# A hybrid decoder layer on one core: the input projection of the prompt's second half moved from the opening in among the expert tokens

## What is computed

```
p = h @ w_in                                  # 1024 -> RWKV r,k,v,w,a,g | GDN q,k,v,z,b,a | gates
ya, ... = rwkv_branch(p_rw, ...)              # token shift, low-rank maps, recurrence over tokens
yb, ... = gdn_branch(p_gd, ...)               # causal_conv of 4 taps, silu, l2norm, delta rule in chunks
merged = gates[..., :D] * (ya @ w_branch_a) + gates[..., D:] * (yb @ w_branch_b)
x1 = layer_norm(alpha * x + merged @ w_out)
...
hpre = einsum('tkd,td->tk', u_tab[e_b], x_b)  # 128 experts a token
y = einsum('tk,tkd->td', g_b * gelu(hpre), v_tab[e_b])
x2 = layer_norm(alpha * x1 + y)
```

## Time and profile before

| | |
|---|---|
| median of 3 runs | 2156.61 us (2156.49 to 2164.32) |
| span of the profiled execution | 2167.9 us |
| TensorE busy | 1626.5 us, 75% |
| VectorE busy | 1336.0 us, 62% |
| ScalarE busy | 398.7 us, 18% |
| GpSimd busy | 1019.4 us, 47% |
| moved by DMA | 718.93 MB, 332 GB/s over the span |

### The profile page before, as it was taken

One profiled execution on the slowest core, in us unless ns is written; L12 is line 12 of the kernel. 1 busy time (PEld: TensorE's weight loads), 2 busy tenths in 40 slices (PEclk: granted clock), 3 DMA queues, 4 the chain that ended last, 5 costly groups with the idle time before them and its releaser, 6 DMA issues. The chain is left out here.

```text
span 2167.9 us, 32130 instructions
## 1 busy us (share of the span) xinstructions
PE 1626.5 (75%) x12765; PEld 974.2 (45%) x12789; DVE 1336.0 (62%) x2996; ACT 398.7 (18%) x754; POOL 1019.4 (47%) x1091
## 2 busy tenths in 40 slices
PE   7998879897978785598888656888776555656555
PEld 7887866864655552065655302666553000100000
DVE  4296177784645458865545777645456875676745
ACT  1321332241222011113401201223012000100000
POOL 0000020004645555665545566645455677777774
PEclk9997999996989996599999756979998555555555
DMA  9214286656999999999999999989999999999997
GB/s 253 77 49 136 80 223 183 225 177 225 358 369 400 399 401 407 377 355 388 394 399 400 412 403 382 383 304 398 399 400 404 401 402 405 406 406 397 406 407 273
DMA packets 271257, 718.93 MB, mean 332 GB/s; under 512 B 29220, under 2 KB 77823, under 8 KB 270075
## 3 DMA queue, kind: packets, MB, share of 16 engines
q0 software_dynamic: 151904, 554.59, 66.3%
q1 hardware_dynamic: 116552, 161.44, 21.7%
q10 hardware_dynamic: 2650, 0.85, 0.2%
HBM read 695.58 MB, written 21.30 MB: 331 GB/s over the span
## 5 line engine op out<-in xcount | busy, mean ns | idle before, releaser
L2558 DVE CUSTOM_DVE_ANT_0 arena<-arena,ps 128x1024 f32<-128x1024 f32 x520 | 634.5, 1220 | 523.1 <-PE ps L2611 331.7
L2458 POOL DMA_INDIRECT arena<-peer_u_dram,arena x520 | 503.2, 968 | 500.6 <-DVE arena L2558 415.9
L2503 POOL DMA_INDIRECT arena<-peer_v_dram,arena x520 | 489.0, 940 | 163.6 <-issue 152.5
L2611 PE MATMUL ps<-arena 48*128 48x512 bf16 x1040 | 264.7, 501 | 338.3 <-DVE arena L2558 325.6
L1318 PE MATMUL ps<-arena 128*128 128x128 f32 (+1 forms) x3072 | 415.7, 291 | 85.9 <-DMA arena<-w_in_dram 35.1
L1318 PEld LDWEIGHTS ps<-arena 128*128 128x128 f32 x3072 | 380.6, 200 | 178.7 <-issue 123.0
L2624 PE MATMUL ps<-arena 128*32 128x512 f32 x2080 | 397.1, 847 | 24.0 <-DMA arena<-peer_v_dram,arena 23.8
L2611 PEld LDWEIGHTS ps<-arena 48*128 48x128 bf16 x1040 | 53.7, 98 | 648.7 <-DVE arena L2558 574.0
L2592 ACT ACTIVATE arena<-arena 128x4 f32<-128x4 f32 x130 | 26.8, 206 | 910.1 <-DVE arena L2558 909.8
L388 PE MATMUL ps<-arena 128*128 128x260 f32 (+1 forms) x704 | 131.7, 349 | 3.9 <-ACT arena L466 3.9
L388 PEld LDWEIGHTS ps<-arena 128*128 128x128 f32 x704 | 116.4, 193 | 18.1 <-ACT arena L466 4.0
(11 more groups left out here) (367 smaller groups left out, 1805.6 us busy)
## 6 DMA issues: line engine op xcount, KB each, us to landing
arena<-w_in_dram SPq DMA_DIRECT2D x40, 1024.0 KB, 13.1
arena<-peer_wq_dram SPq DMA_DIRECT2D x32, 1024.0 KB, 14.6
arena<-w_out_dram SPq DMA_DIRECT2D x16, 1024.0 KB, 15.7
arena<-w_in_dram SPq DMA_DIRECT2D x30, 512.0 KB, 4.1
arena<-peer_u_dram,arena POOLq DMA_INDIRECT x520
arena<-peer_v_dram,arena POOLq DMA_INDIRECT x520
arena<-w_branch_a_dram SPq DMA_DIRECT2D x8, 1024.0 KB, 14.8
arena<-w_branch_b_dram SPq DMA_DIRECT2D x8, 1024.0 KB, 16.7
```

The costliest lines, as they stand in the source:

```text
L2458: pool.indirect_dma_start(m["arena"][:, at:at + D], None, m["a"]["peer_u"][0], offsets(m, k)).then_inc(m["sem"](f"e_u{k % RU // UB}"), 16)
L2503: pool.indirect_dma_start(e["V"][j % RV], None, a["peer_v"][0], offsets(m, j)).then_inc(v_in[j % RV // BATCH], 16)
L2558: dve.tensor_tensor_reduce(u, u, ps[:, 0:2, :], 1.0, 0.0, ALU.mult, ALU.add, e["hp"][:, c:c + 1]).then_inc(sem("e_h"), 1)
L2611: mm = pe.matmul(ps[:, h, :], e["pick"][r, i:i + 1].to_broadcast([3 * GROUP, P]), e["xp"][r, g % 2, :], start=True, stop=True)
```

## The change

The opening projects tiles 0 and 1 and the samples alone, 264 columns, for all 30 tiles of w_in. The late part of the opening goes. Instead the recurrence of tile 0 carries the transposes of x of tiles 2 and 3 and their small GDN inputs (`extra_pe` and its like), and the rest of the projection of tiles 2 and 3 is done in the running stage (`second_*`), 256 columns at a time: the 30 units stand 1.4 tokens apart from token 95 on, their weights come in 15 slabs of 512x512 through a ring of four, and the 11 results are written to `fin`, 22 transfers of 256 KB. Tile 2's recurrence begins at token 141 instead of 118, tile 3's at 249 instead of 244, and some paces of choosing and of the samples are set anew.

```diff
-BEGINS = (-160.0, 3.0, 118.0, 244.0)
-STRETCH = (1.0, 1.0, 1.0, 1.07)
-CHOOSE_PACE = (0.55, 0.58, 0.78, 0.78, 1.2)
+BEGINS = (-160.0, 3.0, 141.0, 249.0)
+STRETCH = (1.0, 1.0, 0.86, 1.02)
+CHOOSE_PACE = (0.4, 0.58, 0.56, 0.7, 1.2)
...
-                    pe.wait_ge(tile_out, i - 1)
-                few = TILES[i] >= RT_
-                for h in range(1 if few else 2):
-                    for k in range(KD):
-                        x = xA[:, k, :] if few else xT[:, k, h * TH:(h + 1) * TH]
-                        mm = pe.matmul(ps[:, 2 * (i % 2) + h, 0:NA if few else TH], ring[:, i % WS, k, :], x, start=(k == 0), stop=(k == KD - 1))
+                if i >= 4:
+                    pe.wait_ge(tile_out, i - 3)
+                for k in range(KD):
+                    mm = pe.matmul(ps[:, i % 4, 0:TA], ring[:, i % WS, k, :], xT[:, k, :], start=(k == 0), stop=(k == KD - 1))
...
-S_AT = dict(rows=33.2, save=38.6, exp=51.2, rw=46.6, gd=52.5, sum0=63.2, gd2=63.6, sum1=76.3, turn=78.5, keys=85.8)
+S_AT = dict(rows=33.2, save=36.0, exp=47.5, rw=44.0, gd=48.5, sum0=51.5, gd2=52.0, sum1=59.5, turn=61.0, keys=63.5)
...
+SB, UNIT = 95.0, 1.4
+SSLOTS = 4
+SECOND_SLABS = [(g, h) for g, n in GROUPS for h in range(1 if n == 2 else 2)]
+SPILLS = ("gk", "gq", "gv", "z", "gg", "A", "B", "R", "K", "bonus", "V")
...
+def second_sp(m, sp):
+
+    a, sem, f = m["a"], m["sem"], m["second"]
+    slabs = [sem(f"p_slab{i}") for i in range(SSLOTS)]
+
+    def slab(s):
+        g, h = SECOND_SLABS[s]
+        c0 = GROUP_ROW[g] * P
+        if s >= SSLOTS:
+            sp.wait_ge(sem("p_mm"), unit_number(SECOND_SLABS[s - SSLOTS][0], dict(GROUPS)[SECOND_SLABS[s - SSLOTS][0]] - 1))
+        if g == "wg":
+            src, here = a["w_in"][0, :, c0:c0 + 256], shaped(flat(f["ring"][s % SSLOTS]), [KD, 256])
         else:
-            pe.wait_ge(out, taken(u - 2))
-
-    def project_late(g):
+            src, here = a["w_in"][0, 512 * h:512 * h + 512, c0:c0 + 512], f["ring"][s % SSLOTS]
+        sp.dma_start(here, src.rearrange("(k p) c -> p k c", p=P)).then_inc(slabs[s % SSLOTS], 16)
...
+                if h == 0 and u > 2:
+                    pe.wait_ge(out, u - 2)
+                slot = f["ring"][s % SSLOTS]
+                for k in range(4):
+                    w = shaped(flat(slot), [KD, 256])[:, 4 * h + k, ct * P:(ct + 1) * P] if n == 2 else slot[:, k, ct * P:(ct + 1) * P]
+                    mm = pe.matmul(ps[:, FB + u % 2, 0:NF], w, f["x"][:, 4 * h + k], start=(h == 0 and k == 0), stop=(h == 1 and k == 3))
...
-            in_turn(recur_r_pe(m, pe, 0), recur_g_pe(m, pe, 0), front_pe(m, pe, 0), sample_pe(m, pe), late_pe(m, pe))
+            in_turn(recur_r_pe(m, pe, 0), recur_g_pe(m, pe, 0), extra_pe(m, pe), front_pe(m, pe, 0), sample_pe(m, pe))
-TURN = (116, 116, 116, 108)
+TURN = (116, 120, 116, 108)
...
 def fin_sp(m, sp, n):
 
     tn = tokens(n)
-    yield front_at(n - 1, "fin")
+    yield front_at(n - 1, "fin") if n > 2 else unit_at("v", 3) + 6.8
     m["fs"].wait(sp, n, "rows", 0)
+    if n == 2:
+        second_done(m, sp)
     sp.dma_start(m["finbuf"][:, 0:NFIN * tn], m["a"]["fin"][n - 1][:, 0:NFIN * tn]).then_inc(m["sem"]("fin_in"), 16)
...
-            in_turn(experts_sp(m, sp), *(s(m, sp, n) for n in later for s in (fin_sp, front_sp, store_sp) if (s, n) != (fin_sp, 1)), states_sp(m, sp), rows_sp(m, sp))
+            in_turn(experts_sp(m, sp), second_sp(m, sp), *(s(m, sp, n) for n in later for s in (fin_sp, front_sp, store_sp) if (s, n) != (fin_sp, 1)), states_sp(m, sp), rows_sp(m, sp))
...
-            in_turn(experts_dve(m, dve), *(s(m, dve, n) for n in later for s in (recur_r_dve, recur_g_dve, front_dve)),
+            m["second_steps"] = Steps(dve, sem("p_step"))
+            in_turn(experts_dve(m, dve), second_dve(m, dve), *(s(m, dve, n) for n in later for s in (recur_r_dve, recur_g_dve, front_dve)),
...
-            in_turn(experts_pe(m, pe), *(s(m, pe, n) for n in later for s in (recur_r_pe, recur_g_pe, front_pe)),
+            in_turn(experts_pe(m, pe), second_pe(m, pe), *(s(m, pe, n) for n in later for s in (recur_r_pe, recur_g_pe, front_pe)),
```

More of the change, by code:

```diff
@@ L216, in program @@
             m[name] = late.take(shape, dt)
[L217 to L232, removed]
+        m["arena"], m["rings_at"] = arena, late.at
+        small_at = expert_rows(m)[2]
+        fin_at = ARENA - NFIN * (P + NS)
+        high = Space(arena, small_at + SMALL, fin_at)
+        for name, n in (("Praw", RT_), ("sw", 4), ("aa", 4), ("G", 4), ("Gi", 4), ("mix", RT_), ("kk", 4), ("scr", 4), ("xT", KD), ("gg", 4),
+                        ("rawA", QT), ("sqA", 8), ("convA", QT), ("zA", ZT)):
+            m[name + "_at"] = high.at
+            m[name] = high.take([P, n, TA])
+        m["Gp"] = m["sw"]
+        m["once_at"] = high.at
+        m["finbuf"] = arena[:, fin_at:ARENA]
+        second = Space(arena, fin_at, ARENA)
+        for name, shape in (("xrowB", [P, 2, D]), ("xTB", [P, KD, NF]), ("wba", [P, KD, BG]), ("lin", [BG, NF]), ("spB", [BG, NF]), ("keep", [P, 2, NF])):
+            m[name] = second.take(shape)
+        early = Space(arena, low.at, small_at)
         m["tmp"] = lambda name, shape, dt=F32: early.take(shape, dt)
@@ L336, in _ @@
         def _(dve):
-            for n in range(NT):
+            for n in range(2):
                 dve.wait_ge(turned, n + 1)
@@ L1010, in recur_g_pe @@
     for h in range(HG):
-        mm = pe.matmul(by4(G + 1)[:, h], selv[0:BG, HG + h], i["bg"], start=True, stop=True)
+        mm = pe.matmul(by4(G + 1)[:, h], row(32 + h), i["bg"], start=True, stop=True)
     mm.then_inc(S_["selg"], 1)
@@ L1025, in recur_g_pe @@
     for h in range(HG):
-        mm = pe.matmul(by4(G + 1)[:, h], selv[0:BG, h], i["bg"], start=True, stop=True)
+        mm = pe.matmul(by4(G + 1)[:, h], row(h), i["bg"], start=True, stop=True)
     mm.then_inc(S_["selb"], 1)
@@ L1270, in front_sp @@
                 sp.wait_ge(m["sem"]("q_kmm"), 2)
-            elif before == "f":
+            else:
                 source, g, h = SLABS[j]
@@ L1707, in opening_buffers @@
+    m["samples"] = s
+    rest = Space(space.arena, own.at, end)
+    f.update(qT=rest.take([P, HP * P]), left=rest.take([P, D]), parts=rest.take([P, 3, D], BF16),
+             scores=shaped(past_mix, [HP, NK]), x1row=past_mix[:, HP * NK:HP * NK + D])
     f["choose"] = {}
@@ new lines, in chain, with merged, extra_pe @@
+def chain(*streams):
+    for s in streams:
+        yield from s
+def merged(*streams):
+    heads = [next(s, None) for s in streams]
+    while any(h is not None for h in heads):
+        i = min((i for i, h in enumerate(heads) if h is not None), key=lambda i: heads[i])
+        yield heads[i]
+        heads[i] = next(streams[i], None)
+def extra_pe(m, pe):
+    ps, sem = m["ps"], m["sem"]
+    yield begins(0) + 4.0
+    pe.wait_ge(sem("xB_in"), 32)
+    for n in range(2):
+        for k in range(KD):
+            mm = pe.transpose(ps[:, 2 * n + k // 4, (k % 4) * P:(k % 4 + 1) * P], m["xrowB"][:, n, k * P:(k + 1) * P], const(m, "ident"))
+            if k % 4 == 3:
+                if k == 7:
+                    mm.then_inc(sem("xB_mm"), 1)
+                yield begins(0) + 4.5 + 1.0 * n + 0.5 * (k // 4)
+    yield begins(0) + 8.0
+    pe.wait_ge(sem("xB_out"), 2)
+    for k in range(KD):
+        mm = pe.matmul(ps[0:BG, 0, 0:NF], m["wba"][:, k, :], m["xTB"][:, k, :], start=(k == 0), stop=(k == KD - 1))
+    mm.then_inc(sem("xB_ba"), 1)
@@ L2467, in clear_small @@
 def clear_small(m, dve):
+    yield begins(0) + 33.0
     e, sem = m["small"], m["sem"]
```

958 lines of the change are left out of this document (528 added, 430 removed).

## The result

The changed kernel is slower: a median of 2238.09 us (2234.73 to 2242.64) against 2160.47 us for the kernel before in the same runs, a ratio of 1.0352 with an interval of 1.0307 to 1.0397. That is 78 us more, where 26 were forecast and the range ended at 2215. The sign was right, the size was not.

What follows compares the result with a forecast made beforehand. The opening was taken as bound by TensorE, the running stage by memory bytes; -62 us in the opening and +88 running (57 + 19 + 8 + 4) gave +26, a median of 2183 us, range 2134 to 2215.

Steps and rivals of the forecast that it cites:

- Opening: Stretch up to the first expert token: loading, projecting, recurrence, front, choosing and end together save 62 us, between 45 and 80.
- Project: Opening's projection: fewer TensorE instructions at 264 columns, with TensorE staying the bound, -25 us (-18 to -32).
- Recurrence: Tile 0's recurrence in the opening: added transposes and matmuls on TensorE cost +10 us (+5 to +14).
- Front up to the first query's scores: Front of tile 0: late groups go, but TensorE waits for the samples' two sums and the keys, -23 us (-15 to -33).
- End: End of the opening: choosing without late work, -8 us, and first expert multiply no longer behind the last late group, -11.
- Bytes: Running stage: 23.1 MB of slabs, x, low-rank weights and spills at 403 GB/s, with no idle DMA to hide them, +57 us.
- +19 in tokens 94 to 116: Running stage: added convolutions and norms make VectorE the bound, +19 us beyond the bytes (0 to +30).
- +8 in 116 to 142: Running stage: TensorE, memory and VectorE near full and chained, +8 us (0 to +20).
- Tile 2's input: Running stage: tile 2's recurrence starts later and its input loads only after the last spill, +4 us (0 to +15).
- (a): Rival: rings of gathered rows absorb the VectorE and TensorE overload, so only bytes count; 2154 us, chance 0.2.
- (b): Rival: samples' chain does not limit the opening, second sum under 65 us after the recurrence; 2132 to 2145 us, chance 0.2.
- (c): Rival: SyncE's queue delays the second projection, pushing tile 2's recurrence and front into its choosing; 2213 us, chance 0.15.

Runs made afterwards that it cites:

- floor run: Changed kernel without the second projection's engine work, slabs, x, low-rank weights and the last states' outputs; only 22 spills of zeros stay: 2131.69 us.
- transfers-only run: Changed kernel without the second projection's work on TensorE, VectorE and ScalarE and the last states' outputs; its transfers stay, spilling zeros: 2174.36 us.
- run of rows alone: The transfers-only run without low-rank weights, plus VectorE's full-width second-projection rows on constants at their old places: 2209.40 us.
- Narrow rows: Changed kernel with nearly all second-projection rows on VectorE cut from 256 columns to 8 or less, zeros spilled: 2205.95 us.
- half of the matmuls: Changed kernel with 4 of 8 matmuls in each of the second projection's 30 units: 2234.32 us alone, 2199.82 us together with narrowed VectorE rows.

## Why the prediction was wrong

**Opening, -62 forecast, -54 measured.** Loading: the first projecting matmul starts at 16.04 us instead of 21.86, -6 (-5). Project: -15 (-25). The last of its main matmuls did come 30 us earlier (149.24 for 179.03, loading included), as the instruction count said; but then TensorE waited 14.43 us for VectorE ahead of the recurrence, where it had waited 3.14. The prediction let the two changes on VectorE cancel; the longer tail is the 10 us. Recurrence: -1 (+10); the added transposes found room in its waits. Front up to the first query's scores: -17 (-23). The mechanism was right: the first sum came 60 us after the front began (61 forecast), the second 88 (85). End: -15 (-19).

**Bytes, +57 forecast.** Right for 17.3 MB, which cost 43 us. For the 5.8 MB of spills, 14 us by the same price, no run shows the price alone: the floor run, which has them, lies 34 us under the kernel before where the opening alone gives 54, and the 20 between hold its wait of 30.0 us for tile 2's input, with tokens that went faster elsewhere.

**The work among the tokens, +19 in tokens 94 to 116 and +8 in 116 to 142: the step that failed.** By the floor runs the work costs 64 us over the transfers, where these two terms allowed 27. By the tokens' starts in the two traces, the changed kernel loses 22 us to the transfers-only run from token 94 to 95, 27 to token 116 and 33 to token 142; some 19 come back behind that, where the transfers-only run has the longer wait for tile 2's input. So the sum failed in three places.

At token 95 it had nothing. x was costed in bytes, not as a transfer that may start only when tile 1's rows have left its buffer, with TensorE and VectorE standing in order behind it. That stage took 27 us; without the wait it takes 5, as before. How much would come back if this wait alone went is not shown, since the runs without it moved other things too.

In tokens 95 to 116 the working was nearly right, and its row was misread. The 56 us from 842 to 898 hold 18 expert multiplies, not the 22 that the prediction takes them for; tokens 95 to 116 took 66 us, with VectorE busy for 57.94 (its row stands in the section on the result). The sizes of the new rows were right: 0.487 us for a multiply-add and 3.351 for a reciprocal of half a norm (0.49 and 3.35 estimated), 38 us in all. 57.94 and 38 are 96, and VectorE was busy for 96.11 us; at the 0.90 of the prediction that is 107 us, and 108 were measured. (The bytes of that sum are slightly low too: 22.8 MB, nine slabs and x are 33 MB, 83 us, still under VectorE's time.) VectorE alone sets this pace: in the run of rows alone, with TensorE's units gone, the same tokens took 104 us.

In tokens 116 to 142 the term of +8 was mis-sized: 33. There VectorE's rows alone cost nothing (87 us with and without them), so the cost needs TensorE's units, ScalarE's evictions and the real spills beside them. VectorE's waits there, from 916 to 1036 us (L2216 and L2229 wait for spills to leave a buffer, L2225 and L2216 for ScalarE):

```profile
DVE arena L2759 <- PE ps L2812: 20.0, 11, 3.6
DVE arena L2216 <- DMA fin_dram<-arena: 10.3, 1, 10.3
DVE arena L2225 <- ACT arena L2146: 5.6, 1, 5.6
DVE arena L2216 <- ACT arena L2109: 5.6, 1, 5.6
DVE arena L2229 <- DMA fin_dram<-arena: 3.0, 1, 3.0
```

Narrow rows returned 11 of the 33 and half of the matmuls 8 more, although the rows alone are free and halving the matmuls alone returned 3, which fits engines that wait for each other in turn. How the other 14 divide between evictions and the waits for spills stays open.

**Tile 2's input, +4.** Tokens 142 to 150 took 29 us more than before, 24 of them this wait. The runs that moved it were 34 to 38 us ahead at token 150 and lost 25 to 44 behind it to a denser choosing or front, so they don't show it as a loss of 20 in the end; its price alone stays open.

**Rivals.** (a), that the overload is absorbed, is refuted by the run of rows alone; (b) by the samples' second sum at 88 us; (c) named the late end, tile 2's load behind the last spill, which came as a wait of 24 us, but another cause: SyncE's queue was not what was waited for, it waited itself, for x's buffer and later for VectorE at a spill; and its 2213 is 25 us short.

No version here that computes the full result beats the kernel before: the opening's 54 us are less than the 57 of bytes before any work is placed.

## What to carry to other kernels

Work moved into a stage that is full in the memory pays its bytes in full; price that first, against the gain, and if the two are near, stop. Then ask of each engine's list over the few items that a ring covers, not over the stage: here the gathered rows of six tokens of `peer_u`; with VectorE busy for 96 of 108 us the gathers waited for it, and the share of the memory fell to 0.80. That a longer ring would have covered it is not shown, for no run changed the ring. A buffer handed from one stage to the next is a wait of its own; find in the listing what must have left it, and who stands behind in order. And read a change of place to the end of the run: what was ahead by 34 to 38 us at token 150 was mostly gone 90 tokens later.

## What the runs showed of the hardware

The price of a byte was not constant. Eleven slabs, 11.5 MB, cost 11 us while all the work stood among them (shares of 0.80 and 0.86): 1 us in tokens 95 to 116 and 11 in 116 to 142. 17.3 MB cost 43 where the share was 1.04.

The granted clock of TensorE stood at 0.50 through the whole transfers-only stretch, its lower level of 1.2 GHz, with 32.17 of 86 us busy; at 0.71 and 0.81 with half of the units' matmuls, and at 0.88 and 0.91 with all of them. So taking matmuls away saved less than their time. From 808 to 916 us the units took 63.16 us with 238 instructions and 42.73 with 116, and TensorE's busy time fell by 14 of 86 us.
